# Dilated attention woven into a projection stream: stops of two query blocks in place of steps of one

## The reference, cut to what matters

```
DIL_PATTERNS = ((128, 1), (512, 4), (2048, 16))     # 12 heads, 4 for each pattern
s = jnp.einsum('brnqhd,brnkhd->brnhqk', qs, kb) * (HEAD_DIM ** -0.5)
valid = (dist >= 0) & (dist <= steps) & (ki[:, None, :] >= 0)
s = jnp.where(valid[None, None, :, None], s, -jnp.inf)
m = jnp.max(s, axis=-1, keepdims=True); e = jnp.exp(s - m); l = jnp.sum(e, axis=-1, keepdims=True)
o = jnp.einsum('brnhqk,brnkhd->brnqhd', e / l, vb);  lse = (m + jnp.log(l))[..., 0]
...
wts = jax.nn.softmax(jnp.stack(lses, axis=0), axis=0)      # over the three patterns
o = jnp.concatenate([outs[g] * wts[g][..., None] for g in range(3)], axis=2)
```

## Time and profile before

| | |
|---|---|
| median of 3 runs | 3193.05 us (3192.22 to 3193.63) |
| span of the profiled execution | 3189.9 us |
| TensorE matmul busy | 3164.3 us, 99% |
| TensorE weight load busy | 2503.5 us, 78% |
| VectorE busy | 2036.2 us, 64% |
| ScalarE busy | 988.1 us, 31% |
| GpSimd busy | 1719.1 us, 54% |
| attention stretch, layer 0 | about 90 to 402 us |
| attention stretch, layer 1 | about 1272 to 1585 us |
| second block's attention | about 2525 to 2773 us |

### The profile page before, as it was taken

One profiled execution on the slowest core, in us unless ns is written; L12 is line 12 of the kernel. 1 busy time (PEld: TensorE's weight loads), 2 busy tenths in 40 slices (PEclk: granted clock), 3 DMA queues, 4 the chain that ended last, 5 costly groups with the idle time before them and its releaser, 6 DMA issues.

```text
span 3189.9 us, 39393 instructions
## 1 busy us (share of the span) xinstructions
PE 3164.3 (99%) x14756; PEld 2503.5 (78%) x14756; DVE 2036.2 (64%) x2749; ACT 988.1 (31%) x1847; POOL 1719.1 (54%) x1544
## 2 busy tenths in 40 slices
PE   8999999999999999999999999999999999999999
PEld 6776788888888888777788888888888767688887
DVE  6546476666666664555476666665758988898323
ACT  3223243333333421222253333332422244402212
POOL 5633356666666446533366666666455534376675
PEclk9999999999999999999999999999999999999999
DMA  5111211111111122112231111112111100011112
GB/s 156 45 42 33 85 55 53 53 54 53 55 53 60 50 88 62 46 33 59 59 62 48 53 53 53 55 53 67 45 47 47 40 27 21 27 49 48 50 53 86
DMA packets 306349, 173.73 MB, mean 54 GB/s; under 512 B 61424, under 2 KB 296944, under 8 KB 306160
## 3 DMA queue, kind: packets, MB, share of 16 engines
q1 hardware_dynamic: 287904, 162.55, 17.7%
q10 hardware_dynamic: 18256, 8.67, 0.9%
HBM read 155.13 MB, written 12.91 MB: 53 GB/s over the span
## 4 chain that ended last, share of the span: by engine, by line
PE 95%; DVE 4%; ACT 1%; issue 0%; DMA 0%; DVEq 0%; ACTq 0%; SPq 0%
PE ring L1252 18%; PE ring L1254 17%; PE ring L1253 17%; PE aux L1252 5%; PE aux L1254 5%; PE aux L1253 5%; PE ring L1495 3%; PE ring L1494 3%; PE ring L1493 3%; PE aux L1493 2%; PE aux L1494 2%; PE aux L1495 2%; PE aux L1346 1%; PE aux L1332 1%; PE aux L1322 1%; PE aux L1600 1%
## 5 line engine op out<-in xcount | busy, mean ns | idle before, releaser
L1001 POOL TENSOR_TENSOR w_hi<-w_raw,ones 128x512 fp32r<-128x512 f32 (+3 forms) x408 | 448.3, 1099 | 917.4 <-PE ring L1254 735.5
L1004 POOL TENSOR_TENSOR w_lo<-w_raw,w_hi 128x512 fp32r<-128x512 f32 (+3 forms) x408 | 541.6, 1327 | 32.0
L1252 PE MATMUL ring<-Q_hi,w_hi 128*128 128x512 f32 x1312 | 519.2, 396 | 0.0
L1254 PE MATMUL ring<-Q_hi,w_lo 128*128 128x512 f32 x1312 | 511.3, 390 | 0.0
L1253 PE MATMUL ring<-Q_lo,w_hi 128*128 128x512 f32 x1312 | 511.2, 390 | 0.0
L1252 PEld LDWEIGHTS ring<-Q_hi,w_hi 128*128 128x128 f32 x1312 | 246.2, 188 | 76.4 <-issue 26.3
L1254 PEld LDWEIGHTS ring<-Q_hi,w_lo 128*128 128x128 f32 x1312 | 246.3, 188 | 52.0
L1253 PEld LDWEIGHTS ring<-Q_lo,w_hi 128*128 128x128 f32 x1312 | 246.4, 188 | 50.3 <-issue 1.0
L1252 PE MATMUL ring<-P_hi,w_hi 128*128 128x512 f32 x656 | 275.8, 420 | 1.6 <-DVE P_lo L2215 1.2
L1254 PE MATMUL ring<-P_hi,w_lo 128*128 128x512 f32 x656 | 257.1, 392 | 0.0
L1253 PE MATMUL ring<-P_lo,w_hi 128*128 128x512 f32 x656 | 257.0, 392 | 0.0
(11 more groups left out here) (397 smaller groups left out, 7063.7 us busy)
## 6 DMA issues: line engine op xcount, KB each, us to landing
w_raw<-in_w_in SPq DMA_DIRECT2D x84, 512.0 KB, 3.8
w_raw<-in_w_up SPq DMA_DIRECT2D x64, 512.0 KB, 4.0
w_raw<-in_w_down SPq DMA_DIRECT2D x64, 512.0 KB, 3.4
h_scratch<-h ACTq DMA_DIRECT2D x16, 512.0 KB, 3.7
w_raw<-in_w_gate SPq DMA_DIRECT2D x16, 512.0 KB, 3.9
hx<-h_scratch SPq DMA_DIRECT2D x12, 512.0 KB, 6.5
x_raw<-in_x SPq DMA_DIRECT2D x8, 512.0 KB, 7.8
w_raw<-in_w_out SPq DMA_DIRECT2D x16, 256.0 KB, 2.9
```

Source lines behind the costliest of these rows:

```text
L1001: g.tensor_tensor(w_hi[:, slot, ks], w_raw[:, slot, ks], one.broadcast_to([P, width, P]), ALU.mult).then_inc(w_hi_ready, 1)
L1004: g.tensor_tensor(w_lo[:, slot, ks], w_raw[:, slot, ks], w_hi[:, slot, ks].bitcast(F32), ALU.subtract).then_inc(w_ready, 1)
L1252: t.matmul(o, wh, xh, start=first, stop=False)
L1254: return t.matmul(o, wl, xh, start=False, stop=last)
```

## The change

A unit has four *stops* of two query blocks each in place of eight steps of one. They stand 10 chunks apart (7 for unit 5), the first at chunk 11 of the unit's six halves. The lag is still two, now of stops. In a stop TensorE turns the pair before, then scores this pair, then attends the pair two stops back, for all parts at once. VectorE takes both blocks' scores first and copies the turned probabilities of both after that; ScalarE copies both attended blocks, once both are there, and then takes the exponentials. For this the scores use both halves of their banks, `probs_t` and the turned probabilities get a second buffer (the latter is bank 2), and the halves of the attention stretch alternate between banks 0 and 1 alone. VectorE's copy now also waits for the attend of the same buffer before (`attended`), and the first half of part B waits for the last copy.

Two more edits: the spread contracts over all 128 rows in place of 38 (with `rows` cleared on all of them), and in a step of the second block TensorE turns the weights of all parts first, then meets, then scores.

```diff
-    return (0, 1, 2, 6, 7)[m % 5] if m < (10 if l < DEPTH else 20) else m % 3
+    if m < (10 if l < DEPTH else 20):
+        return (0, 1, 2, 6, 7)[m % 5]
+    return m % 2 if l < DEPTH and m < 2 * PART_B else m % 3
...
-STEPS, LAG = 8, 2
+STEPS, STOPS, LAG = 8, 4, 2
+def pair_of(i):
+    return 2 * i, 2 * i + 1
...
-        for s in range(STEPS):
-            put(m0 + 1 + s // 2, 2 + 4 * (s % 2), "step", unit, s)
+        for i in range(STOPS):
+            k = 11 + 10 * i
+            put(m0 + k // KC, k % KC, "step", unit, i)
...
-    for s in range(STEPS + LAG):
-        put_a(8 + 3 * s, "step", 5, s)
+    for i in range(STOPS + LAG):
+        put_a(8 + 7 * i, "step", 5, i)
...
-    side, scores, turned, attend_bank = bank[3], bank[4:6], bank[6], bank[7]
+    side, scores, turned, attend_bank = bank[3], bank[4:6], (bank[6], bank[2]), bank[7]
...
+        def attention_stop(l, parts):                    # TensorE
+            for unit, i in parts:
+                if 1 <= i <= STOPS:
+                    for j in pair_of(i - 1):
+                        turn_probs(l, unit, j)
+            for unit, i in parts:
+                if i < STOPS:
+                    for j in pair_of(i):
+                        score_block(l, unit, j)
+            for unit, i in parts:
+                if i >= 2:
+                    for j in pair_of(i - 2):
+                        attend(l, unit, j)
...
-            t.matmul(side, sel[0:38, g], rows[0:38, :], start=True, stop=True).then_inc(side_done, 1)
+            t.matmul(side, sel[:, g], rows[:], start=True, stop=True).then_inc(side_done, 1)
...
+            elif l < DEPTH and m == 2 * PART_B:
+                pe.wait_ge(probs_taken, (l + 1) * UNITS * STEPS)
...
                     for c, u in step_parts(*args):       # TensorE, second block
+                        if TURN_LAG <= u < len(ROUNDS) + TURN_LAG:
+                            turn_weights(c, u - TURN_LAG)
+                    for c, u in step_parts(*args):
                         if meets_after(u) is not None:
                             meet(c, meets_after(u))
-                        if TURN_LAG <= u < len(ROUNDS) + TURN_LAG:
-                            turn_weights(c, u - TURN_LAG)
+                    for c, u in step_parts(*args):
                         if u < len(ROUNDS):
                             score(c, u)
...
         def take_probs(l, unit, j):                      # VectorE
-            dve.wait_ge(probs_turned, step_no(l, unit, j) + 1)
+            dve.wait_ge(probs_turned, no + 1)
+            if no >= 2:
+                dve.wait_ge(attended, no - 1)
...
-            dve.wait_ge(scored, at + 1)
+            dve.wait_ge(scored, step_no(l, unit, s | 1) + 1)
...
-                    for unit, s in unit_parts(*args):
-                        if 1 <= s <= STEPS:
-                            take_probs(l, unit, s - 1)
-                        if s < STEPS:
-                            take_scores(l, unit, s)
+                    for unit, i in unit_parts(*args):
+                        if i < STOPS:
+                            for j in pair_of(i):
+                                take_scores(l, unit, j)
+                    for unit, i in unit_parts(*args):
+                        if 1 <= i <= STOPS:
+                            for j in pair_of(i - 1):
+                                take_probs(l, unit, j)
```

More of the change, by code:

```diff
@@ new lines, in turn_probs, with attend @@
+        def turn_probs(l, unit, j):
+            g, no = unit % GROUPS, step_no(l, unit, j)
+            pe.wait_ge(exped, 2 * no + 2)
+            if no >= 2:
+                pe.wait_ge(probs_taken, no - 1)
+            for e in range(2):
+                for b in range(2 if has_prev(g, j) else 1):
+                    mm = t.transpose(turned[j % 2][:, 256 * e + b * P:256 * e + b * P + P], probs[:, j % 2, e, b * P:b * P + P], ident[:])
+            mm.then_inc(probs_turned, 1)
+        def attend(l, unit, j):
+            g, buf, no, cols = unit % GROUPS, unit % 2, step_no(l, unit, j), slice(j % 2 * P, j % 2 * P + P)
+            pe.wait_ge(probs_taken, no + 1)
+            if no and j % 2 == 0:
+                pe.wait_ge(attn_taken, no)
+            blocks = (j - 1, j) if has_prev(g, j) else (j,)
+            for e in range(2):
+                rows = slice(64 * e, 64 * e + 64)
+                for b, jj in enumerate(blocks):
+                    mm = t.matmul(attend_bank[rows, cols], v_t[buf][:, jj, rows],
+                                  probs_t[:, j % 2, e, b * P:b * P + P], start=(b == 0), stop=(b == len(blocks) - 1))
+            mm.then_inc(attended, 1)
@@ new lines, in score_block @@
+        def score_block(l, unit, j):
+            g, buf, no, at = unit % GROUPS, unit % 2, step_no(l, unit, j), j % 2 * 256
+            if j == 0:
+                pe.wait_ge(rotated, l * ROTATIONS + 4 * unit + 4)
+                if unit == 0:
+                    pe.wait_ge(summed, sum_no(l, Y_HN2, 0, 0))
+            if no and j % 2 == 0:
+                pe.wait_ge(masked, 2 * no)
+            first = j - 1 if has_prev(g, j) else j
+            for e in range(2):
+                rows = slice(64 * e, 64 * e + 64)
+                mm = t.matmul(scores[e][:, at:at + (j + 1 - first) * P], q_t[buf][rows, j * P:j * P + P],
+                              k_t[buf][rows, first * P:(j + 1) * P], start=True, stop=True)
+            mm.then_inc(scored, 1)
@@ L1390, in woven @@
                 elif kind == "step":
-                    for part in unit_parts(*args):
-                        attention_step(l, *part)
+                    attention_stop(l, unit_parts(*args))
                 elif kind == "pool":
@@ new lines, in exp_block @@
+        def exp_block(l, unit, j):
+            c, g = divmod(unit, GROUPS)
+            n = 2 * P if has_prev(g, j) else P
+            act.wait_ge(max_ready, step_no(l, unit, j) + 1)
+            for e in range(2):
+                x_ = probs[:, j % 2, e, 0:n]
+                a.activation(x_, x_, ACT.Exp, scale=SCALE, bias=neg_max[:, j % 2, e:e + 1],
+                             accum_out=row_stat[:, unit, j, 2 + e:3 + e]).then_inc(exped, 1)
+            if j == STEPS - 1:
+                act.wait_ge(exped, 2 * step_no(l, unit, j) + 2)
+                to = stats_d[l, c]
@@ new lines, in exp_block, with attention_stop @@
+                    act.dma_start(to.rearrange("(n p r) g f -> p r n g f", n=2, r=4)[:, :, :, 1],
+                                  row_stat[:, unit].rearrange("p (r n) f -> p r n f", n=2)).then_inc(stats_out, 16)
+                else:
+                    for q in range(2):
+                        act.dma_start(to.rearrange("(i j q) g f -> q i j g f", j=8, q=2)[q][:, :, 2],
+                                      row_stat[64 * q:64 * q + 64, unit]).then_inc(stats_out, 16)
+        def attention_stop(l, unit, i):
+            if i >= 2:
+                for j in pair_of(i - 2):
+                    take_attended(l, unit, j)
+            if i < STOPS:
+                for j in pair_of(i):
+                    exp_block(l, unit, j)
@@ L2317, in share_weights @@
             if c == 0:
-                v.memset(rows[0:38, :].bitcast(F32), 0.0).then_inc(rows_empty, 1)
+                v.memset(rows[:].bitcast(F32), 0.0).then_inc(rows_empty, 1)
             dve.wait_ge(stats_in, 16 * (2 * l + c + 1))
```

94 lines of the change are left out of this document (22 added, 72 removed).

## The result

The changed kernel takes 3168.12 us (median of 4 runs, 3166.05 to 3170.20) against 3193.34 us of the kernel before: a ratio of 0.9924, interval 0.9912 to 0.9936. It is faster, by 25 us where 45 were forecast. The profiled execution spans 3167.6 us against 3189.9, 22.3 less.

A forecast was written before the change was run, and what follows sets the result against it. TensorE's queue was taken to bound the kernel, with 95% of the last chain. Terms -41 - 6.9 - 2.6 - 2.0 + 6.0 + 1.4 = -45.1 put the span at 3144.8 and the time at 3148 us, range 3138 to 3163.

The forecast's parts named there:

- Stops, -41: TensorE's attention insertions: two-block stops pay 0.55 us of fixed tile-shape changes where two steps paid 1.42; 41 us less.
- The unknown term: TensorE's change from scores to attends within a stop, absent from the earlier trace: taken as 0.15 us, range 0 to 0.20.
- Spread, -6.9: The 24 spreads on TensorE: 128 rows save 0.39 us each, only partly in chunk 1; 6.9 us less together.
- Waits that go, -2.6: TensorE's waits at layer 1's first turn, each layer's fourth turn and chunk 1's turn_w disappear; 2.6 us less.
- Two banks, 0: Attention halves alternating between two banks instead of three: VectorE frees each in time, by 0.8 us in unit 3; no cost.
- The rival that put the change on the slow side: VectorE needs 2 us more at each of 48 stops, so TensorE waits for banks; 3201 us, chance 0.05.
- VectorE's pieces, +6.0 and +1.4: VectorE takes each stop in one piece, delaying woven work: 6.0 us more in unit 3's halves, 1.4 at pool matmuls.
- turn_w at 0.6 us a layer: In unit 3's halves, TensorE waits 0.6 us at chunk 0's turn_w for VectorE's weights, with shares taking 2.4 us.
- Turn before meet, -2.0: Second block: one tile-shape change fewer at each of 15 meets, 0.15 us each; booked as 2.0 us less.
- One of the prediction's own signs of being wrong: TensorE's idle time in the two attention stretches exceeding some 12 us would show the prediction wrong.
- The rival of weight loads (3158): Second block of a stop: the second score pair's two weight loads show, 9.6 us more; 3158 us, chance 0.12.
- VectorE later: Unit-end halves: VectorE's short operations stretch, each of 12 halves adding 1 to 1.5 us; 3163 us, chance 0.10.

The follow-up runs named there:

- the base kernel: The changed kernel with the second block's meet before the turn again and chunk 0's shares placed ahead of the unit's first stop on VectorE: 3150.19 us.
- the second placement: The base kernel with most of chunk 0's spreads 1 to 4 chunks later, unit 5's turns of v 2 later, chunk 1's spreads three apart: 3150.60 us.

## Why the prediction was right in its direction and 20 us short

1. *Stops, -41.* Right in its mechanism, and 2.3 us too much. Stops of 128 and 256 columns cost 1.87 and 3.21 us where 1.85 and 3.15 follow from the prices. All insertions together fell by 40.3, of which 1.6 are waits at turns that part 3 books, so 38.7 are the stops. The unknown term, scores to attends at 0.15, was measured from both sides (a stop with one more change 0.15 dearer, with three more 0.5). The Trainium skill says of TensorE that changing the tiling mode drains the engine (TensorEngine Tiling (Array Packing), Key Properties); these runs agree and put 0.14 to 0.17 us on each change added within a stop.
2. *Spread, -6.9.* Right: -6.9 measured alone. That chunk 1 keeps half of it was an estimate that held.
3. *Waits that go, -2.6.* Right: neither the turns (1.6 before) nor turn_w of chunk 1 (0.6 before) wait.
4. *Two banks, 0.* Nearly right, with little to spare: the waits for a half that VectorE has not read are 0.6 us in the kernel after. They are 2.8 in the base kernel, 1.4 in one layer and 1.5 in the other, each behind an addition that lasts 2.03 us beside a GpSimd operation: such a stretch is longer than the 0.8 us to spare. They are 4.4 as soon as VectorE's piece ends about 1 us later (attends first, copies first). The rival that put the change on the slow side had a mechanism that exists, at few stops instead of all.
5. *VectorE's pieces, +6.0 and +1.4.* The rows (1.7 us, twice) and the pool matmuls (1.5) are as forecast. The weighing is 2.8 in six places where I had 0.9 in two: 0.8 in chunk 0, and 2.0 in chunk 1, which I had booked as a smaller gain of part 2. The run with the spreads alone waits for the same 2.0. **The step that failed is the first wait, turn_w at 0.6 us a layer: it was 4.4.** The working gave `shares` its duration from the earlier trace rows, 2.4 us. There GpSimd was idle; the change moves `shares` against TensorE, GpSimd splits weights when TensorE gives a slot free, and the two fell together. The forecast had times of TensorE and VectorE in it and none of GpSimd. With GpSimd's work taken away the wait is 0.9. The trace of before held the warning: chunk 1's shares already ran beside GpSimd there. Timeline of VectorE and GpSimd in the kernel before, one of their operations, which takes 0.21 us when GpSimd is idle:

```profile
370.08 0.92 DVE L2324 TENSOR_TENSOR share<-read_back,top 128x48 f32<-128x48 f32 x1
```

```profile
369.88 1.04 POOL L1004 TENSOR_TENSOR w_lo<-w_raw,w_hi 128x384 fp32r<-128x384 f32 x1
```

6. *The clock was not in the sum.* A wait of 4.4 us cost another 2 (4.1 for two, by the difference of run times), since the chip granted TensorE the lower level during it and for 4.7 us behind it (5.0 in layer 1). Behind the spread's 1.7 us no lower clock shows; behind the 2.6 us of the second placement it does. Behind the two waits of 2.0 in the tail of the second block it shows in the kernel after, and behind the same two in the kernel before with the turn first it doesn't.
7. *Turn before meet, -2.0.* **Wrong in sign: +5.4 alone, +4.8 within the change.** The change of shape is worth the 0.15 that was booked, but it came off at seven meets of 15. I had asked whether ScalarE's sigmoids come later and found 1 us to spare. In the tail VectorE sets the pace, and there the meet was what TensorE did while it waited; at three meets before the tail it waits 0.41 too. Costing the edit at nothing but the change of shape left out the work that hid a wait.

Together: turn_w 7.6 us, its clock 4.1, the meet 4.8 + 2.0, the sum 18.5 of the 20 missing in the run times, and 20.8 with the stops' 2.3. In the spans 22.8 are missing (22.3 less where the sum has 45.1). The 3.15 that the prediction added for the run times is the median less the span of one execution; a run stands only 1.8 above its own span (3169.38 and 3167.6), and with 1.8 the forecast would have been 3146.6. The base kernel, without these two faults, is 41.5 us faster than its kernel before, where the sum without the meet's 2.0 and the 1.2 at turn_w gives 44.3; the stops' 2.3 lie between. That its 3150.2 stands beside the forecast's 3148 is in small part luck.

One of the prediction's own signs of being wrong came true: the waits of TensorE in the attention stretches are 8.8 + 3.4 + 2.8 + 1.5 + 0.6 = 17.1 us, over the 12 that it allowed.

The rival of weight loads (3158) falls: a second score pair adds only its streaming (eight score records at 198.50 last 0.71 us, four in the earlier trace rows 0.49, the difference being 0.22 for 128 columns more). The rival *VectorE later* was the nearest to the truth in time and cause, and the evidence that it rested on was already the mechanism: the maximum of 2.40 us in the earlier trace rows has a GpSimd operation beside it in the trace of before (timeline of GpSimd):

```profile
1273.43 2.39 POOL L1076 TENSOR_TENSOR pool_u<-mix,pool_u 128x1024 f32<-128x1024 f32 x1
```

Both end at 1275.8. I had read the row as chance, "short operations stretch at times", and not looked at the engine beside it.

## What to carry to other kernels

Before a short VectorE operation on SBUF is moved, look at what GpSimd does at its new place, and bound its duration by what is left of GpSimd's operation and its own together. A matmul that seems free to move may be the filler of someone's wait: price it in the stretch where the other engine sets the pace. And where a wait is moved away, follow everything that shares its bank and everything behind it on the releasing engine, or it comes back under another name, as it did twice here before 9 us were had.

## What the hardware showed

- VectorE's operations with two inputs in SBUF, and the scaling of two maxima with one, last as if they waited for the GpSimd operation that was running when they began: they end behind its end by what they take alone, less some 0.14 us. The rows: operations of 16 and 48 columns, 0.17 and 0.21 alone, end 0.03 and 0.07 behind it; in the kernel before the additions of 512 columns (L2477), 0.69 alone, end 0.55 behind it in all 42 places, and last 1.78 to 2.56; the operations of 1024 columns on the weights of the second block (L2676), 1.23 alone, end 1.08 behind it. Operations that read one input from PSUM don't show it: the masked scores of 256 columns (L2340) take 0.41 to 0.43 us in the kernel after, in 32 places beside GpSimd as in 56 others.
- The reverse shows too: in the base kernel GpSimd's w_hi took 1.48 us where it began during a subtraction of VectorE's (246.80 and 246.91), and 1.04 otherwise. The Trainium skill states both as an exclusive lock on a shared pair of ports, taken by whoever comes first, where VectorE has two SBUF inputs or runs in a two-port mode (SBUF — State Buffer, SBUF: two separate sides). The traces agree, with the times given here.
- A matmul that uses 38 of 128 rows between full ones costs 0.62 us, one that uses all 128 costs 0.24.
- A wait costs TensorE more than its length where the granted clock falls with it: 4.55 us of late start cost 6.6 in all (13.2 for two in plain times, 12.4 by the ratios).
